# Feeding the mixers un-normed transposed rows, with the bias table's repetition moved from the SyncE queue to a memory-to-memory copy

## The chip, the cores and the metric

The kernel runs on one core of one Trainium2 chip. The metric is the device time of one execution in microseconds; the kernel before has a median of 1729.02 us over 3 runs (1727.54 to 1730.34). The core has TensorE (matmuls and transposes), VectorE, ScalarE and GpSimd for elementwise work, SyncE, which here only issues transfers, and 16 DMA engines that all queues share.

## What is computed

A decoder trunk of two layers on 256 tokens of width 1024, in float32. Each layer: (1) a norm of the residual `h`, one input projection, three token mixers that share it (a diagonal state space scan, latent attention, sparse attention), an output projection; (2) cross-attention into 256 memory tokens `mem`; (3) a SwiGLU channel mixer, dense in layer 0 and with eight experts in layer 1. What the change touches is this:

```python
def rmsnorm(x, g):
    y = xf * lax.rsqrt(jnp.mean(xf * xf, axis=-1, keepdims=True) + EPS)
    return (y * g.astype(jnp.float32)).astype(x.dtype)
...
for l in range(DEPTH):
    proj = rmsnorm(h, mix_norm[l]) @ w_in[l]
    u, cq, ckv, kr, nq, nkv, ngate = jnp.split(proj, offsets, axis=-1)
    y_ssm = ssm_mixer(u, ...)      # complex powers of a, scan over tokens
    y_mla = mla_mixer(cq, ckv, kr, ...)
    y_nsa = nsa_mixer(nq, nkv, ngate, ..., rel_bias)   # scores get head_bias(q_pos - k_pos)
    h = h + concat(norms of y) @ w_out[l]
    h = h + cross_attn(h, mem, ...)
    h = h + (swiglu or moe)(rmsnorm(h, ffn_norm[l]))
```

The scale of the norm is one number per token, so it commutes with the projection: it can be applied to `h` before or to `proj` after.

## The kernel before, in words

**Products and weight chunks.** Every product of the large matrices is made in three matmuls of rounded operands (`split_product`, L456 to L458): each operand is an upper part (rounded) and a lower part (the rest). Weights come in chunks of 1 MB into a ring of six slots, all issued by SyncE, in order, each once the slot's last user is done (semaphore `weights_used`). For each chunk ScalarE writes the upper part (`layer_chunk_upper`, L476) and VectorE the lower part (`layer_chunk_lower`, L480); TensorE waits for the lower one in `split_chunk`. The upper part of chunk c also waits for the user of chunk c-2. Engines run their instructions strictly in the order written; nothing reorders the work.

**Input of a layer.** The squares of `h` (ScalarE L1673 in layer 0, VectorE L1898 in layer 1), a mean, a power on GpSimd (L2350) and a scaling by `rstd` give `row`; TensorE turns it into columns (L1232, 16 transposes `hT0` to `hT3` into banks 0 to 3); ScalarE and VectorE evict the columns times `mix_norm` as upper (`colr`, L1642) and lower (`coll`, L1908) part. Then come the jobs `u`, `zA`, `zB`, `q0`, `q1` (chunks 0 to 4), `ck` and `cv` (chunk 5) and `vs` (chunk 6). Each job is 48 matmuls. Banks go round in fives, each job waiting until the bank's last job is drained.

**After the jobs.** TensorE makes `hid` (L1375, the compression of the sparse group) and `bu0` (L1339, the scan's input). VectorE writes `memr` (L2078), the lower part of the memory columns, in place over `memraw`, then drains `hid`, then does `states(0)` (from 76.5 us in the rows) and so on to the scores.

**GpSimd, layer 0.** Two powers, and a table of complex powers by doubling (`tables`, then `double(1)` to `double(128)`, six operations each over 8m elements, L2350; it needs the sines of L1654). After the last doubling it issues two transfers: `mem_cols` (the memory columns to memory, L2394, `memory_columns` in the profile, 1 MB; semaphore `mem_kept`, for which `memr` waits) and `btab` (L2397), a skewed read of the bias. Both go by GpSimd's own queue.

**The bias.** A small matmul (L1301) makes 6 rows of 384 numbers, VectorE copies them to `biasrow` in SBUF, and SyncE writes each row 128 times to `scratch` in memory (L1195, `skewed_bias`), ahead of chunk 6 in SyncE's queue.

**Between the layers.** The last dense product adds into banks 0 to 3, VectorE adds them to `h` (L943, four times 128x512), and the input of layer 1 begins. ScalarE copies the next layer's powers from `row` and `col` into `big` there (L1681, L1682).

Of the kernel before, what the change touches and what calls it, by code (L numbers as in the profile page):

```python
# [84 lines left out]
JOBS = []  # L85

# [7 lines left out]
for _i, (_n, _e) in enumerate((("u", "act"), ("zA", "act"), ("zB", "act"), ("q0", "dve"), ("q1", "dve"))):  # L94
    _job(_n, _e, _i)
_job("ck", "act")
# [99 lines left out]
def trunk(nc, x, mem, weights, lparams, consts, onehot, relb, fgain, out, scratch, routed, expert_out, mem_cols):  # L196
    with ExitStack() as ctx:
# [50 lines left out]
        eight = sb("eight", [P, 16])  # L248

# [8 lines left out]
        colr = over("colr", [P, KD, T], "col")  # L258
        memr = over("memr", [P, KD, T], "memraw")
# [32 lines left out]
        ftab = big  # L292
# [40 lines left out]
        xsc = small[:, 440:442]  # L333

# [15 lines left out]
        s_out = sem("s_out")  # L350
        bias_back = sem("bias_back")
        mem_kept = sem("mem_kept")
# [21 lines left out]
        row_ready = lsem("row_ready")  # L374
        mem_upper = lsem("mem_upper")
# [45 lines left out]
        def bank(name):  # L421
            return banks[index(name) % ROT]
# [84 lines left out]
        def dense_pe(pe, last_rows, last_columns):  # L507
# [32 lines left out]
            def down(i, n, start=False, last=False):  # L540
                q = f0 + (3 * i + 2 if last else 3 * i + 4)
                pe.wait_ge(split_done, 3 * n + (3 if last else 5))
                pe.wait_ge(hT_done, n + 1)
                up, lo = upper[:, third(q), :], lower[:, q % RING, :]
                for f in range(2):
                    for t in range(TT):
                        x = slice(f * T + t * P, f * T + (t + 1) * P)
                        for nn in range(2):
                            w = slice(f * 1024 + nn * 512, f * 1024 + (nn + 1) * 512)
                            ins = split_product(pe, banks[2 * t + nn][:, :], htu[:, i % 2, x], htl[:, i % 2, x],  # L550
                                                up[:, w], lo[:, w], start and f == 0, last and f == 1)
                ins.then_inc(weights_used, 1)
# [19 lines left out]
            down(n, n, last=True)  # L572
            pe.wait_ge(weights_used, RING + LAYER_CHUNKS)
# [52 lines left out]
        def moe_pe(pe, m, used, first):  # L626
# [34 lines left out]
            def gather_first():  # L661

                pe.wait_ge(row_ready[1], 6)
# [231 lines left out]
        def dense_dve(dve, last_half, next_angles):  # L895
# [37 lines left out]
            step(1, 2 * e + 1, e)  # L933
            step(DENSE_PIECES - 3, DENSE_PIECES - 3)
            step(DENSE_PIECES - 2, DENSE_PIECES - 2, chunks=1)
            units(DENSE_PIECES - 1, DENSE_PIECES - 1)
            for c in range(2):
                layer_chunk_lower(dve, 1, c)
            dve.wait_ge(weights_used, RING + LAYER_CHUNKS)
            for t in range(TT):  # L940
                for n in range(2):
# [160 lines left out]
        def moe_pool(pool, m, tile):  # L1102
# [12 lines left out]
            pool.wait_ge(row_ready[1], 6)  # L1115
# [101 lines left out]
        def _(pe):  # L1217
# [82 lines left out]
            pe.wait_ge(p_dve, 1)  # L1300
            mm(banks[7][0:NH, 0:384], pt[0:33, 1, 0:NH], pt[0:33, 0, 0:384], start=True, stop=True).then_inc(p_pe, 1)  # L1301
            pe.wait_ge(cst_landed, 16)

            def turn_memory(i):

                if i == 0:
                    pe.wait_ge(p_dve, 2)
                    pe.wait_ge(p_act, 3)
                if i == 3:
                    pe.wait_ge(p_act, 4)  # L1310
# [6 lines left out]
            for l in range(L):  # L1317
                pe.wait_ge(row_ready[l], 2)
                transpose_rows("h")
                features_out("u", 0, colr, coll, "h")  # L1320
                narrow_tokens_out("zA", 1, colr, coll)
                narrow_tokens_out("zB", 2, colr, coll)
                features_out("q0", 3, colr, coll)
# [3 lines left out]
                features_out("q1", 4, colr, coll)  # L1327
                if l == 0:
                    turn_memory(3)
                for v, name in enumerate(("ck", "cv")):  # L1330
                    half_features_out(name, 5, v, colr, coll)
                narrow_tokens_out("vs", 6, colr, coll)
# [168 lines left out]
                for i in range(HEADS):  # L1501
                    if scored_at(i):
                        scores(*scored_at(i))
                    if i in MEMK:
                        if MEMK[i] == 0:
                            pe.wait_ge(mem_split[l], KD)
                        features_out(f"mk{MEMK[i]}", MEM_FIRST + MEMK[i], colr, memr)
# [25 lines left out]
                tokens_out("mv0", MEM_VALUES, colr, memr)  # L1533
                tokens_out("mv1", MEM_VALUES + 2, colr, memr, (0,))
                pe.wait_ge(row_ready[l], 4)
                transpose_rows("y", row, (0, 1))
                tokens_out("mv1", MEM_VALUES + 2, colr, memr, (1,))
# [63 lines left out]
                if l == 0:  # L1601
                    wait_drained(pe, l, "fT1")
                    dense_pe(pe, last_rows, last_columns)
# [14 lines left out]
        def _(act):  # L1618
# [11 lines left out]

            def scale_rows(n):

                act.wait_ge(rstd_ready[l], n)
                A(row[:, 0, :], h[:, 0, :], ACT.Copy, scale=rstd[:, 0:1]).then_inc(row_ready[l], 1)
# [36 lines left out]
            act.wait_ge(x_landed, 16)  # L1671
            for t in range(TT):
                ins = A(xkf[:, t * D:(t + 1) * D], h[:, t, :], ACT.Square, accum_out=ss[:, t:t + 1])  # L1673
            ins.then_inc(p_act, 1)
            trigonometry(0)

            for l in range(L):
                if l:
                    act.wait_ge(weights_used, RING + LAYER_CHUNKS)
                    act.wait_ge(ftab_ready[l], 1)  # L1680
                    A(bigf[:, 2048:4096], rowf, ACT.Copy).then_inc(ftab_ready[l], 1)  # L1681
                    A(bigf[:, 0:2048], colf, ACT.Copy).then_inc(ftab_ready[l], 1)  # L1682
                    act.wait_ge(ftab_ready[l], 3)
                    scale_rows(1)
                else:
                    layer_chunk_upper(act, 0, 0)
                transposes_upper(l, "h", C_MIX)
                if l == 0:
                    layer_chunk_upper(act, 0, 1)
                wait_tile(act, l, "u")  # L1690
                layer_chunk_upper(act, l, 2)
                drained(A(uT[:, :, :], bank("u")[:, :], ACT.Copy))
                wait_tile(act, l, "zA")
                layer_chunk_upper(act, l, 3)
                drained(A(z[:, :, 0:256], bank("zA")[:, :].rearrange("p (t n) -> p t n", t=2), ACT.Copy))
# [3 lines left out]
                A(z[:, :, 256:352], b[:, :, 0:96], ACT.Copy)  # L1699
                A(gates, b[:, :, 96:114], ACT.Tanh, scale=0.5)  # L1700
                drained(A(kwr[:, :, :], b[:, :, 114:242], ACT.Copy))
# [10 lines left out]
                wait_tile(act, l, "ck")  # L1712
                for gi in range(2):
                    b = bank("ck")[gi * 64:(gi + 1) * 64, 0:T]
                    A(kc[0:64, 0, gi, :], b, ACT.Copy)
                    ins = A(kc[64:128, 0, gi, 0:255], b[:, 1:256], ACT.Copy)
                drained(ins)
# [8 lines left out]
                else:  # L1726
                    act.wait_ge(p_act, 7)
                for k in range(KD):
                    A(colr[:, k, :], memraw[:, k, :], ACT.Copy, scale=cols[:, C_MEM + k:C_MEM + k + 1]).then_inc(mem_upper[l], 1)
# [5 lines left out]
                act.wait_ge(ftab_ready[l], 2 * l + 1)  # L1735
# [142 lines left out]
        def _(dve):  # L1878
# [34 lines left out]
            def norm_h(junk, l):  # L1913
                for t in range(TT):
                    if l:
                        dve.wait_ge(ffn_added, 2 * t + 2)
                    ins = squares(h[:, t, :], junk[:, t * D:(t + 1) * D], ss[:, t:t + 1])
                link(ins)
                mean_eps(0, 2, D).then_inc(ss_ready[l], 1)

            def scale_rows(n):

                dve.wait_ge(rstd_ready[l], n)
                if l:
                    dve.wait_ge(ftab_ready[l], 3)
                dve.tensor_scalar(row[:, 1, :], h[:, 1, :], rstd[:, 1:2], None, ALU.mult).then_inc(row_ready[l], 1)

# [27 lines left out]
            angles(0)  # L1955
            dve.wait_ge(bias_landed, 32)
            dve.tensor_scalar(pt[0:33, 1, 0:NH], pt[0:33, 1, 0:NH], 8.0, None, ALU.mult).then_inc(p_dve, 1)

            for l in range(L):
                if l:  # L1960
                    norm_h(xkf, l)
                    scale_rows(1)
                else:
                    dve.wait_ge(p_act, 1)
                    mean_eps(0, 2, D).then_inc(ss_ready[l], 1)
                    dve.wait_ge(rstd_ready[l], 1)
                    for t in range(TT):
                        dve.tensor_scalar(row[:, t, :], h[:, t, :], rstd[:, t:t + 1], None, ALU.mult).then_inc(row_ready[l], 1)
                    dve.wait_ge(p_pe, 1)
                    dve.tensor_copy(biasrow, banks[7][0:NH, 0:384]).then_inc(p_dve, 1)  # L1970
                    layer_chunk_lower(dve, l, 0)
                transposes_lower("h", coll, C_MIX, 0)
                if l == 0:
                    layer_chunk_lower(dve, l, 1)
# [663 lines left out]
```

## Time and profile before

| | |
|---|---|
| median of 3 runs | 1729.02 us |
| the profiled execution's own time | 1730.89 us |
| its span, first to last instruction | 1729.1 us |
| mean granted TensorE clock | 0.982 of full speed |
| TensorE matmul busy | 1660.1 us, 96% |
| VectorE / ScalarE / GpSimd busy | 1347.5 / 1087.3 / 225.2 us |

All times below are microseconds from the span's start in that one execution. A matmul's ends are modelled, so that TensorE's waits are read from the engine that released it and from the chain of work, not from its busy share.

### The profile page before, as it was taken

The numbers are of one execution on the slowest core, as the hardware profiler recorded it, in microseconds if no ns is written. First come the engines' busy times: TensorE is split into PE (matmuls) and PEld (weight loads), VectorE is DVE, ScalarE is ACT, GpSimd is POOL, SyncE is SP. The second block draws the span as 40 slices with busy tenths as digits, with TensorE's granted clock in tenths as the row PEclk, the third lists the DMA queues.
The fourth block names the chain that finished last, engine by engine and source line by source line (L and its number), as shares of the span: only waits on it lengthen the run. The fifth ranks groups of instructions, "written<-read, shape, count | busy, mean of one in ns | idle before, by whom it ended". The sixth has DMA issues, their size and how long they took to land.

```text
span 1729.1 us, 24273 instructions
## 1 busy us (share of the span) xinstructions
PE 1660.1 (96%) x8480; PEld 1386.1 (80%) x8480; DVE 1347.5 (78%) x1501; ACT 1087.3 (63%) x1195; POOL 225.2 (13%) x235
## 2 busy tenths in 40 slices
PE   7899999999799999999999999999999999999995
PEld 6788888888697888878888888888888888888783
DVE  7676656445667756678988988988989889889895
ACT  5455544445445554367777777777777777777773
POOL 7443001003603500040000000000000000000200
PEclk9889999999998999989999999999999999999998
DMA  8602526855440234379999999999999999999992
GB/s 297 239 25 74 181 111 232 337 179 189 170 147 25 74 128 165 122 281 399 377 373 378 379 381 374 370 391 372 385 375 376 384 371 362 388 373 360 418 372 75
DMA packets 68111, 475.94 MB, mean 275 GB/s; under 512 B 7533, under 2 KB 8301, under 8 KB 13390
## 3 DMA queue, kind: packets, MB, share of 16 engines
q1 hardware_dynamic: 62790, 452.11, 68.7%
q0 software_dynamic: 5024, 22.86, 3.4%
q8 instruction: 39, 0.64, 0.1%
q10 hardware_dynamic: 232, 0.12, 0.0%
q14 instruction: 26, 0.21, 0.0%
HBM read 461.82 MB, written 13.24 MB: 275 GB/s over the span
## 4 chain that ended last, share of the span: by engine, by line
PE 83%; DVE 6%; ACT 4%; DMA 4%; issue 2%; POOL 0%; DVEq 0%; POOLq 0%; ACTq 0%; SPq 0%
PE bank L456 24%; PE bank L458 24%; PE bank L457 24%; DMA ring<-in_weights 3%; ACT upper L499 1%; PE bank L647 1%; DVE lower L480 1%; ACT upper L476 1%; PE bank L1339 1%; PE bank L1554 1%; DVE xel L1014 1%; PE bank L1455 1%; DVE lower L505 1%; PE bank L1513 1%; PE bank L1232 1%
## 5 line engine op out<-in xcount | busy, mean ns | idle before, releaser
L505 DVE TENSOR_TENSOR lower<-ring,upper 128x2048 fp32r<-128x2048 f32 x369 | 849.3, 2302 | 145.0 <-ACT upper L499 132.2
L499 ACT ACTIVATE upper<-ring 128x2048 fp32r<-128x2048 f32 x369 | 706.2, 1914 | 113.5 <-PE bank L458 100.9
L456 PE MATMUL bank<-upper,xeu 128*128 128x512 f32 x896 | 360.0, 402 | 3.5 <-DVE lower L505 3.5
L458 PE MATMUL bank<-upper,xel 128*128 128x512 f32 x896 | 350.5, 391 | 0.0
L457 PE MATMUL bank<-lower,xeu 128*128 128x512 f32 x896 | 349.5, 390 | 0.0
L456 PE MATMUL bank<-upper,htu 128*128 128x512 f32 x536 | 209.9, 392 | 4.9 <-DVE htl L1030 3.4
L458 PE MATMUL bank<-upper,htl 128*128 128x512 f32 x536 | 208.7, 389 | 0.0
L457 PE MATMUL bank<-lower,htu 128*128 128x512 f32 x536 | 208.6, 389 | 0.0
L456 PEld LDWEIGHTS bank<-upper,xeu 128*128 128x128 f32 x896 | 168.3, 188 | 36.3 <-DVE lower L505 5.1
L458 PEld LDWEIGHTS bank<-upper,xel 128*128 128x128 f32 x896 | 168.2, 188 | 36.0
L457 PEld LDWEIGHTS bank<-lower,xeu 128*128 128x128 f32 x896 | 168.7, 188 | 31.7
L480 DVE TENSOR_TENSOR lower<-ring,upper 128x2048 fp32r<-128x2048 f32 x42 | 96.7, 2303 | 64.7 <-ACT upper L476 64.3
L456 PEld LDWEIGHTS bank<-upper,htu 128*128 128x128 f32 x536 | 100.6, 188 | 30.9 <-issue 10.5
L476 ACT ACTIVATE upper<-ring 128x2048 fp32r<-128x2048 f32 x42 | 80.3, 1911 | 62.8 <-PE bank L458 62.8
L458 PEld LDWEIGHTS bank<-upper,htl 128*128 128x128 f32 x536 | 100.6, 188 | 21.1
L457 PEld LDWEIGHTS bank<-lower,htu 128*128 128x128 f32 x536 | 100.6, 188 | 20.5
L458 PE MATMUL bank<-colr,lower 128*128 128x256 f32 x384 | 108.7, 283 | 0.0
L824 ACT ACTIVATE htu<-bank 128x256 fp32r<-128x256 f32 x112 | 43.5, 388 | 97.1 <-PE bank L647 96.6
L820 ACT ACTIVATE big<-bank 128x256 f32<-128x256 f32 x112 | 43.0, 384 | 63.8 <-PE bank L458 63.8
L457 PE MATMUL bank<-lower,colr 128*128 128x512 f32 (+1 forms) x224 | 77.9, 348 | 0.0
L458 PE MATMUL bank<-upper,coll 128*128 128x512 f32 (+1 forms) x208 | 77.7, 374 | 0.0
L456 PE MATMUL bank<-colr,upper 128*128 128x256 f32 x256 | 74.4, 291 | 2.7 <-DVE xor L1908 1.8
(387 smaller groups left out, 2474.5 us busy)
## 6 DMA issues: line engine op xcount, KB each, us to landing
ring<-in_weights SPq DMA_DIRECT2D x423, 1024.0 KB, 5.6
routed_rows<-g POOLq DMA_DIRECT2D x1, 4096.0 KB, 36.6
lp<-in_lparams POOLq DMA_DIRECT2D x1, 3634.5 KB, 14.4
lp<-in_lparams SPq DMA_DIRECT2D x1, 3584.0 KB, 35.6
memraw<-routed_rows POOLq DMA_DIRECT2D x7, 512.0 KB, 8.0
expert_rows<-xk POOLq DMA_DIRECT2D x7, 512.0 KB, 9.0
skewed_bias<-vm SPq DMA_DIRECT2D x1, 1152.0 KB
h<-in_x SPq DMA_DIRECT2D x1, 1024.0 KB, 5.7
```

Of the source, the lines that this page charges most:

```text
L456: pe.matmul(to, x_up, w_up, start=start, stop=False, skip_group_check=True)
L457: pe.matmul(to, x_up, w_lo, start=False, stop=False, skip_group_check=True)
L458: return pe.matmul(to, x_lo, w_up, start=False, stop=stop, skip_group_check=True)
L476: act.activation(upper_slot(c), ring[:, c % RING, :], ACT.Copy).then_inc(wt_upper[l], 1)
L480: dve.tensor_tensor(lower[:, c % RING, :], ring[:, c % RING, :], f32(upper_slot(c)), ALU.subtract).then_inc(wt_split[l], 1)
L499: act.activation(upper[:, third(q), :], ring[:, q % RING, :], ACT.Copy).then_inc(done, 1)
L505: dve.tensor_tensor(lower[:, q % RING, :], ring[:, q % RING, :], f32(upper[:, third(q), :]), ALU.subtract).then_inc(done, 1)
L647: ins = pe.transpose(banks[2][:, f * P:(f + 1) * P], hr[:, i % 2, 0, f * P:(f + 1) * P], ident)
L820: act.activation(gs[:, i % 2, 0, :], banks[i % 2][:, 0:256], ACT.Silu).then_inc(m["silu"], 1)
L824: act.activation(htu[:, i % 2, 0:256], banks[2][:, 0:256], ACT.Copy).then_inc(m["ht_up"], 1)
L1014: ins = dve.scalar_tensor_tensor(xel[buf][:, k, :], banks[5 + k // 4][:, (k % 4) * P:(k % 4 + 1) * P], cols[:, C_FFN + k:C_FFN + k + 1], f ...
L1232: ins = pe.transpose(b[:, (k * TT + t) * P:(k * TT + t + 1) * P], src[:, t, f:f + P], ident)
```

## The change

- `h` is turned as it is; `rstd` goes to the drains. A diagonal of `rstd` times a matrix of ones gives a row of it in every partition (`rows_bc`): two matmuls put between `zA` and `zB`, after which VectorE copies the row, drains `u`, and only then makes chunk 2's lower part.
- The turned columns get banks 5, 6, 7, 4, and in layer 1 another place (`bigr` in `big`), so that one of ScalarE's table copies goes. `ck` and `u` are drained by VectorE instead of ScalarE.
- The last dense product goes bank by bank, with the adds and the transposes behind each.
- The bias rows go to memory once (`biasline`); GpSimd repeats them from memory to memory, ahead of `double(64)`.
- In layer 0 the squares, the sines, the factors (L1984 and the lines around it) and the powers on GpSimd come in another order; in layer 1 the factors are made within the dense stage. SyncE loads the identity, then `x`, chunk 0, the other constants.

```diff
 # SyncE
+            sp.dma_start(ident, consts[:, 0:P]).then_inc(cst_landed, 16)
             sp.dma_start(h[:, :, :], x...).then_inc(x_landed, 16)
-            sp.dma_start(cst[:, :], consts).then_inc(cst_landed, 16)
...
                 load(s, s)
+                if s == 0:
+                    sp.wait_ge(cst_landed, 16)
+                    sp.dma_start(cst[:, P:], consts[:, P:]).then_inc(cst_landed, 16)
...
             sp.wait_ge(p_dve, 2)
-            sp.dma_start(scratch[:, :, :], biasrow.unsqueeze(1).broadcast_to([NH, P, 384])).then_inc(s_scr, 16)
+            sp.dma_start(biasline[:, :], biasrow).then_inc(s_scr, 16)
             load(RING, RING)
 # TensorE, per layer
-                pe.wait_ge(row_ready[l], 2)
-                transpose_rows("h")
+                if l == 0:
+                    pe.wait_ge(x_landed, 16)
+                    transpose_rows("h", h)
+                    ... the bias matmul, into bank 3
+                else:
+                    last_down()
+                    for n in range(2):
+                        for t in range(TT):
+                            pe.wait_ge(ffn_added, 2 * n + t + 1)
+                            turn_blocks("h", h, (2 * n, 2 * n + 1), t)
+                features_out("u", 0, xh, coll, "h")
+                narrow_tokens_out("zA", 1, xh, coll)
+                pe.wait_ge(diagonal_ready[l], 1)
+                for t in range(TT):
+                    ins = mm(banks[5][:, t * P:(t + 1) * P], ones, pt[:, 0, t * P:(t + 1) * P], start=True, stop=True)
+                ins.then_inc(rows_spread[l], 1)
+                narrow_tokens_out("zB", 2, xh, coll)
 # ScalarE, layer 0
+                    transposes_upper(l, "h", C_MIX, (0, 1))
                     layer_chunk_upper(act, 0, 0)
+                    transposes_upper(l, "h", C_MIX, (2, 3))
+                    trigonometry(0)
+                    layer_chunk_upper(act, 0, 1)
+                    row_squares()
 # VectorE, per layer
+                layer_chunk_lower(dve, l, 1)
+                dve.wait_ge(squared[l], 1)
+                mean_eps(0, 2, D).then_inc(ss_ready[l], 1)
+                if l == 0:
+                    input_factors(0)
+                dve.wait_ge(rstd_ready[l], 1)
+                dve.tensor_scalar(rstd_half, rstd[:, 0:2], 0.5, None, ALU.mult)
+                for t in range(TT):
+                    ins = dve.tensor_scalar(pt[:, 0, t * P:(t + 1) * P], ident, rstd[:, t:t + 1], None, ALU.mult)
+                ins.then_inc(diagonal_ready[l], 1)
+                dve.wait_ge(rows_spread[l], 1)
+                spread = dve.tensor_copy(rows_bc[:, :], banks[5][:, 0:T])
...
+                wait_tile(dve, l, "u")
+                drained(tt(uT[:, :, :], bank("u")[:, :]..., rows_bc[:, :]..., ALU.mult))
+                layer_chunk_lower(dve, l, 2)
+                if l == 0:
+                    ... the squares of the memory rows
+                layer_chunk_lower(dve, l, 3)
 # GpSimd, layer 0
+                    tables(0, *ftab[0], kTf[:, 512:])
+                    for m in (1, 2, 4):
+                        link(double(m))
                 pool.wait_ge(ss_ready[l], 1)
                 power(0, 2, rstd_ready[l])
-                    tables(0, ftab[:, 0], ftab[:, 1], kTf[:, 512:])
-                    for m in (1, 2, 4, 8, 16, 32):
+                    for m in (8, 16, 32):
                         link(double(m))
                     pool.wait_ge(p_dve, 3)
                     power(6, 2, p_pool)
+                    pool.wait_ge(s_scr, 16)
+                    pool.dma_start(scratch[:, :, :], biasline.unsqueeze(1).broadcast_to([NH, P, 384])).then_inc(bias_spread, 16)
                     link(double(64))
                 ...
                     double(128).then_inc(ftab_ready[l], 1)
                     pool.dma_start(mem_cols, memrawf).then_inc(mem_kept, 16)
-                    pool.wait_ge(s_scr, 16)
+                    pool.wait_ge(bias_spread, 16)
                     pool.dma_start(btab[:, :, :], skew).then_inc(bias_back, 16)
```

## Rows read from the trace of the kernel before

**Rows 1.** The page: shares of the chain that ended last.
```profile
PE 83%; DVE 6%; ACT 4%; DMA 4%; issue 2%; POOL 0%; DVEq 0%; POOLq 0%; ACTq 0%; SPq 0%
```

**Rows 2.** The chain in order of time, its longest pieces: start, length, what.
```profile
21.69 35.06 DMA ring<-in_weights
...
58.71 2.30 DVE lower L480
```

**Rows 3.** Stretches: length, busy PE, PEld, DVE, ACT, POOL, clock, DMA share, GB/s.
```profile
25.00:32.00 7.00, 7.00 (x61) 7.00 (x60) 6.62 (x17) 2.40 (x2) 6.68 (x10) 1.00 0.39 61
53.40:61.00 7.60, 0.00 (x0) 0.00 (x0) 2.29 (x2) 4.21 (x7) 5.55 (x4) 0.65 0.82 326
```

**Rows 4.** Timeline of SyncE's queue; then DMA packets by size, 26:31, 52:54, 54:56.
```profile
11.65 0.95 SPq L1195 DMA_DIRECT2D skewed_bias<-vm  x1
21.69 9.50 SPq L1182 DMA_DIRECT2D ring<-in_weights  x1
...
DMA packets 172, 0.26 MB, mean 53 GB/s; under 512 B 0, under 2 KB 172, under 8 KB 172
q1 hardware_dynamic: 172, 0.26, 34.5%
...
DMA packets 100, 0.50 MB, mean 248 GB/s; under 512 B 16, under 2 KB 45, under 8 KB 45
...
DMA packets 101, 0.79 MB, mean 395 GB/s; under 512 B 7, under 2 KB 7, under 8 KB 7
```

**Rows 5.** Timeline of VectorE: start, length, instructions, idle before and its releaser.
```profile
69.20 0.69 DVE L2054 COPY vs<-bank 128x512 f32<-128x512 f32 x1
71.11 3.26 DVE L2078 SCALAR_TENSOR_TENSOR memr<-memraw,lp,colr 128x256 fp32r<-128x256 f32 x8 [1.22 <-DMA memory_columns<-memraw]
75.49 0.22 DVE L2083 COPY rt<-bank 64x1 f32<-64x1 f32 x2 [1.12 <-PE bank L1375]
76.55 1.29 DVE L1895 TENSOR_TENSOR lp<-bank,big 128x512 f32<-128x512 f32 x2 [0.41 <-PE bank L1339]
```

**Rows 6.** Timelines of ScalarE and GpSimd, layer 0's opening.
```profile
8.76 1.28 ACT L1653 ACT_TABLE_LOAD   x1
...
10.43 0.19 POOL L2363 COPY big<-small 128x8 f32<-128x8 f32 x1 [0.73 <-ACT small L1654]
12.53 2.13 POOL L2350 TENSOR_TENSOR big<-big 128x16 f32<-128x16 f32 x1
14.62 0.21 POOL L2350 TENSOR_TENSOR g<-big 128x16 f32<-128x16 f32 x1
56.13 2.35 POOL L2350 TENSOR_TENSOR big<-big,attn 128x1024 f32<-128x1024 f32 x1
60.45 0.78 POOL L2394 DMA_DIRECT2D memory_columns<-memraw  x1 [1.98 <-ACT memraw L1664]
```

**Rows 7.** DMA issues: KB each, median us to landing.
```profile
h<-in_x SPq DMA_DIRECT2D x1, 1024.0 KB, 5.7
memory_columns<-memraw POOLq DMA_DIRECT2D x1, 1024.0 KB, 10.6
out<-row SPq DMA_DIRECT2D x1, 1024.0 KB, 4.0
```

**Rows 8.** Timelines of TensorE, VectorE, ScalarE where layer 1 begins.
```profile
448.08 0.60 PE L537 MATMUL bank<-cst,big 128*128 128x128 f32 x4
...
467.30 2.48 DVE L943 TENSOR_TENSOR h<-h,bank 128x512 f32<-128x512 f32 x4 [0.30 <-PE bank L458]
474.46 3.65 PE L1232 MATMUL bank<-cst,row 128*128 128x128 f32 x16 [7.20 <-ACT row L1634]
475.58 3.40 ACT L1642 ACTIVATE colr<-bank,lp 128x256 fp32r<-128x256 f32 x8 [1.27 <-PE bank L1232]
484.36 1.92 ACT L476 ACTIVATE colu<-ring 128x2048 fp32r<-128x2048 f32 x1 [5.38 <-PE bank L458]
490.12 1.92 ACT L476 ACTIVATE upper<-ring 128x2048 fp32r<-128x2048 f32 x1 [3.36 <-PE bank L458]
```

More of the change, by code:

```diff
@@ L571, in dense_pe, with last_down @@
             turn(n, n)
-            down(n, n, last=True)
-            pe.wait_ge(weights_used, RING + LAYER_CHUNKS)
+            def last_down():
+                q = f0 + 3 * n + 2
+                pe.wait_ge(split_done, 3 * n + 3)
+                pe.wait_ge(hT_done, n + 1)
+                up, lo = upper[:, third(q), :], lower[:, q % RING, :]
+                for nn in range(2):
+                    for t in range(TT):
+                        for f in range(2):
+                            x = slice(f * T + t * P, f * T + (t + 1) * P)
+                            w = slice(f * 1024 + nn * 512, f * 1024 + (nn + 1) * 512)
+                            ins = split_product(pe, banks[2 * t + nn][:, :], htu[:, n % 2, x], htl[:, n % 2, x],
+                                                up[:, w], lo[:, w], False, f == 1)
+                        ins.then_inc(weights_used if (nn, t) == (1, TT - 1) else dense_done, 1)
+            return last_down
         lg = bigf[:, 3072:3088].rearrange("p (t e) -> p t e", t=TT)
@@ L1953, in angles, with input_factors @@
                 dve.tensor_scalar(ab, ab, 1.0, math.pi / 2, ALU.mult, ALU.add).then_inc(par_ready[l], 1)
[L1955 to L1974, printed above, removed]
-                    dve.wait_ge(mem_landed, 16)
-                    for t in range(TT):
-                        link(squares(memrows[:, t, :], btabf[:, 0:D], ss[:, 6 + t:7 + t]))
-                    mean_eps(6, 2, D).then_inc(p_dve, 1)
-                layer_chunk_lower(dve, l, 2)
+            def input_factors(l):
                 tt(den, lr, lr, ALU.mult)
@@ L1996, in _ @@
                 link(tt(fi, fi, den, ALU.mult))
+            angles(0)
+            dve.wait_ge(bias_landed, 32)
+            dve.tensor_scalar(pt[0:33, 1, 0:NH], pt[0:33, 1, 0:NH], 8.0, None, ALU.mult).then_inc(p_dve, 1)
+            for l in range(L):
+                xh = columns[l]
+                if l:
+                    transposes_lower("h", coll, C_MIX, 0, up=xh)
+                else:
+                    transposes_lower("h", coll, C_MIX, 0, (0, 1))
+                    layer_chunk_lower(dve, l, 0)
+                    transposes_lower("h", coll, C_MIX, 0, (2, 3))
+                    dve.wait_ge(p_pe, 1)
+                    dve.tensor_copy(biasrow, banks[3][0:NH, 0:384]).then_inc(p_dve, 1)
+                layer_chunk_lower(dve, l, 1)
[5 more added lines that the diff above has]
+                dve.tensor_scalar(rstd_half, rstd[:, 0:2], 0.5, None, ALU.mult)
+                for t in range(TT):
+                    ins = dve.tensor_scalar(pt[:, 0, t * P:(t + 1) * P], ident, rstd[:, t:t + 1], None, ALU.mult)
+                ins.then_inc(diagonal_ready[l], 1)
+                dve.wait_ge(rows_spread[l], 1)
+                spread = dve.tensor_copy(rows_bc[:, :], banks[5][:, 0:T])
+                if l == 0:
+                    spread.then_inc(rows_read, 1)
+                    dve.wait_ge(rows_read, 1)
+                else:
+                    link(spread)
+                wait_tile(dve, l, "u")
+                drained(tt(uT[:, :, :], bank("u")[:, :].rearrange("p (c n) -> p c n", c=2),
+                           rows_bc[:, :].unsqueeze(1).broadcast_to([P, 2, T]), ALU.mult))
+                layer_chunk_lower(dve, l, 2)
+                if l == 0:
+                    dve.wait_ge(mem_landed, 16)
+                    for t in range(TT):
+                        link(squares(memrows[:, t, :], btabf[:, 0:D], ss[:, 6 + t:7 + t]))
+                    mean_eps(6, 2, D).then_inc(p_dve, 1)
                 layer_chunk_lower(dve, l, 3)
@@ L2053, in _ @@
                 wait_tile(dve, l, "vs")
-                drained(dve.tensor_copy(vs[:, :, :], bank("vs")[:, :].rearrange("p (t n) -> p t n", t=2)))
+                for t in range(TT):
+                    ins = dve.tensor_scalar(vs[:, t, :], bank("vs")[:, t * 256:(t + 1) * 256], rstd[:, t:t + 1], None, ALU.mult)
+                drained(ins)
                 def states(j):
```

191 lines of the change are left out of this document (97 added, 94 removed).

## The prediction, as it was made before the run

> **What bounds the kernel now.** I read the page's chain of work first: TensorE is 83% of it [rows 1]. So only places where that chain leaves TensorE can give or cost time, and the edits lie at two of them: the opening of layer 0 and the change of layers. I then asked for the chain in order of time, for stretches, and for each engine's timeline around both places.
>
> *Opening.* The longest single piece of the chain is the load of weight chunk 6: issued at 21.69, landed 35.06 us later [rows 2]. `vs` needs it, and TensorE does nothing in 53.4 to 61.0 [rows 3]. The reader should see why it was late. In 25 to 32 the DMA engines move 61 GB/s at a share of 0.39 [rows 3]. In 26 to 31 all 172 packets are under 2 KB (0.26 MB, 1.5 KB each: the bias rows), and they occupy 34.5% of 16 engines, 5.5 engines' worth [rows 4]. The destination is [6, 128, 384]: six engines carry it, 6 x 128 = 768 packets. Chunk 6 stands behind it in the same queue; SyncE even needs 9.50 us to issue it. Such packets are gone between 54 and 56 (45 - 16 = 29 in 52:54, 7 - 7 = 0 after) [rows 4], and then chunk 6 lands.
>
> But VectorE, not TensorE, leads what follows. It has drained `vs` at 69.9 and waits for `memory_columns` until 71.11, writes `memr` for 3.26, waits 1.12 for L1375, and begins `states(0)` at 76.55 [rows 5]. The transfer it waited for comes last in GpSimd's chain: doublings until 58.48, a wait of 1.98 for the memory columns, issue at 60.45 [rows 6], 10.6 to landing [rows 7]. So there are two limits 1 to 2 us apart, and the change removes the first.
>
> *Change of layers.* The last dense matmul ends at 467.3. Four adds, the squares, the power and the scaling follow one another until the transposes at 474.46 [rows 8]: 7.2 us without TensorE.
>
> **The change of layers, step by step.**
> Removed: squares, power and scaling ahead of the transposes. The last dense product is bank by bank, so three of the four adds (2.48 / 4 = 0.62 each [rows 8]) go beside it and the fourth ends at about 468.0. Twelve transposes need not wait for it. After a busy TensorE one takes 0.60 / 4 = 0.15 at most, and 3.65 / 16 = 0.23 now [rows 8]; all are done by about 469.2. ScalarE evicts from 468.0 at 3.40 / 8 = 0.43 per column block, VectorE 0.9 behind it, so the last lower block is there at 472.3, and `u` ends 24 matmuls after the first half, at about 475.9. Before, it ended just ahead of ScalarE's chunk 2 at 484.36, say 484.0 [rows 8]. Gain 8.1. ScalarE's table copy that remains fits ahead of 468, as the one that goes did not have to; the factors put into the dense stage hide beside its matmuls, since there VectorE waits for ScalarE before most chunks (at nothing; uncovered they would be 2.5 us).
>
> Added: a wait that takes part of it back. `zB` needs chunk 2's lower part, and VectorE is written to make that only after the spread row, which TensorE makes only after `zA`. From the end of `zA` (475.9 + 490.12 - 484.36 = 481.7): two matmuls 0.3, a copy of 256 elements 0.45, `u` drained 0.7 (512 elements, as `vs` 0.69 [rows 5]), some 0.1 of links, the lower part 2.3 [rows 2]. TensorE idles about 3.9 us. All behind `zB` on TensorE waits with it; none did before. Net +8.1 - 3.9 = +4.2 for layer 1 (bounds +1.8, if the pause brings the lower clock and its 2.4, and +5). `ck`, and products in place of copies, add about 3 us of work to VectorE, which has as much room before `vs`, as the factors are gone from there.
>
> **The opening, step by step.**
> Same stall of 3.9 between `zA` and `zB`, against 2 us gained by turning `x` before its squares. Chunk 6 now meets a queue with only 9 KB of bias ahead; it should land at about 26 to 30, and `vs` ends at about 61.3 instead of 69.2. Were TensorE the limit, that would be 7.9.
>
> GpSimd's chain is what counts. It starts after the sines. These now follow the transposes of `x`, all eight evictions and chunk 0 on ScalarE. `x` is there at about 6.9 (5.7 to landing [rows 7], issued behind the identity), its first columns at 7.9 (four transposes at 0.23); 8 x 0.43 for the evictions, 1.9 for chunk 0, 1.8 for the sines with their table load of 1.28 [rows 6] make 15.0, against 10.43: 4.6 later. From there to 58.48: a power in the middle +0.7, the issue of the repetition +0.9 (as 0.78 [rows 6]). Beside a lower part on VectorE a GpSimd operation of 0.21 took 2.13 [rows 6]: chunk 0's no longer meets the doublings (-1.9), chunk 6's now does (+2.1). The doublings end at 58.48 + 6.4 = 64.9, and `memory_columns` goes out at about 65. Landing takes 4.0 (1 MB, quiet queues) to 10.6 [rows 7]: 69 to 76.
>
> Now the repetition itself: still 768 packets, issued by GpSimd at about 41, ahead of `memory_columns` in the same queue. Nothing in the trace shows a memory-to-memory copy; the nearest rows are the old transfer's, from about 24.5 to 54, 29.5 us [rows 3, 4]. From below, at 172 packets in 5 us, 22.3 us. From above, 29.5 plus four 1 MB weight chunks sharing the engines at some 2.6 us each: 40. It ends at 41 + 22 to 41 + 40 = 63 to 81, and where it ends last the columns behind it land some 3.5 later. I take the old transfer's 29.5 and half of the sharing, as the shape is the same: end 73, landing T = 76.5.
>
> In the Trainium skill, page "DMA: Bandwidth & Descriptors", section "Why a DMA increments its semaphore by 16 and not by 1", a transfer is split over the largest count up to 16 that divides its outermost dimension, from either kind of queue; by that rule the copy again has six engines. The trace agrees for the old transfer (5.5 engines' worth); no row shows it for GpSimd's queue.
>
> Then `states(0)` begins at T + 3.26 + 0.9 = 80.7, against 76.55: a loss of 4.1. Besides, TensorE has little to do between 68 and 80, and may return at its lower clock. After the pause of 53.4 to 61.0 (mean 0.65 [rows 3]: the lower level, 1.2 GHz, in part of it) `vs` took from 61.0 to 69.2, 8.2, where a job takes 490.12 - 484.36 = 5.76 [rows 2, 5, 8]: 2.4 dearer. So 0 to 2.4; I take 2.
>
> **Sum.** +4.2 - 4.1 - 2.0 = -1.9, a loss. Against the profiled execution's own 1730.89 (span 1729.1) that is 1732.8; that execution lies 1.87 above the median, so on the median 1729.02 + 1.9 = 1730.9.
>
> **Rivals.**
> *Fast: the repetition is out of the way.* It has 16 engines or is quick from memory, and T is 70 to 72. Then layer 0 gives 76.55 - T - 4.2 = +2.3 to +0.3, layer 1 +4.2: 1722.5 to 1725. For it: 16 engines would need 48 packets each. Against it: the unchanged shape. Could the full 7.9 + 4.2 = 12 come (1717)? Only if `memory_columns` landed by 65, when it is about to be issued.
> *Slow: the repetition holds the columns.* From memory to memory each packet reads and writes memory, and shares six engines with weight chunks: end 81 or later, T = 84 to 87, so layer 0 loses 12 to 15, with the clock's 2 and layer 1's 4.2: 1739 to 1742. It decides from T = 78.0 (4.2 = T - 72.35 + 2 - 3.46 turned slower by over 0.2%). For it: 81 is my upper bound. Against: chunks come in bursts with pauses.
> *No change:* the wait for `zB` absent or doubled by a fall of the clock, the rest at zero: within 2 us of 1729.
>
> **How the numbers follow.** A measurement of this kernel tells 0.2% (3.46 us) from no change. Likeliest, T 73 to 78: chance 0.38, 1727.4 to 1732.4, all within 0.2%. No change: 0.03, within it too. Fast: 0.26, faster. Slow, from T = 78 on: 0.33, slower. So faster 0.26, same 0.41, slower 0.33. The range leaves 2 in 10 outside, the far ends of fast and slow: 1723 to 1739.
>
> **What would show it right or wrong.** Chunk 6 landed by 30 and no idle TensorE before `vs`; TensorE idle 3 to 5 us ahead of `zB` in both layers, with VectorE at L480's chunk 2 as releaser; `u` of layer 1 ending 8 us after the last dense matmul's end; GpSimd's last doubling ending at 63 to 67; packets of 1.5 KB in GpSimd's queue until past 65 on about six engines; VectorE's `memr` waiting for `memory_columns`, the longest wait of the opening. Wrong if those packets are over by 55, if GpSimd ends before 60, or if VectorE's own load sets `states(0)`.

## The result, and the profile after

The changed kernel takes 1737.13 us (median of 16 runs, 1730.88 to 1740.39) and the kernel before, beside it, 1729.83 (16 runs, 1727.54 to 1731.9): ratio 1.004, 95% interval 1.0034 to 1.0047. It is 7.3 us slower. The prediction said 1730.9 with a range of 1723 to 1739: the range holds the time, the single figure is 6.2 too low, and "within 0.2%" was the wrong one of the three outcomes. The profiled execution of after took 1736.06 (span 1734.2) against 1730.89 (span 1729.1), so the profile has 5.2 of the 7.3 to explain.

The method below is to look for one event in both traces and to see how the distance between them changes along the span. Four events do: the start of `states(0)`, the last dense matmul, ScalarE's chunk 2 of layer 1 (the end of `u`), and its chunk 4 of layer 1 (the end of `zB`).

**Layer 0's opening: 3.0 later.** The timeline of VectorE in after, where [rows 5] answer to it (start, length, instructions, idle before and its releaser):

```profile
58.53 2.00 DVE L1940 TENSOR_TENSOR rt<-row,cst 128x32 f32<-128x32 f32 x2
60.57 2.34 DVE L1940 TENSOR_TENSOR row<-rt 128x32 f32<-128x32 f32 x1
62.95 2.41 DVE L1940 TENSOR_TENSOR rt<-row,cst 128x32 f32<-128x32 f32 x2
65.39 0.19 DVE L1940 TENSOR_TENSOR row<-rt 128x32 f32<-128x32 f32 x1
...
66.83 3.47 DVE L1940 TENSOR_TENSOR attn<-bank,rows_bc 64x256 f32<-64x256 f32 x8
...
73.68 3.26 DVE L2130 SCALAR_TENSOR_TENSOR memr<-memraw,lp,colr 128x256 fp32r<-128x256 f32 x8 [0.21 <-DMA memory_columns<-memraw]
...
79.52 1.29 DVE L1940 TENSOR_TENSOR lp<-bank,big 128x512 f32<-128x512 f32 x2 [1.36 <-PE bank L1386]
```

`states(0)` starts at 79.52 against 76.55. The wait for `memory_columns` before `memr` is only 0.21, where it was 1.22; the columns are not what is late. The reader should look at the rotation of the shared key's rows (four groups of 128x32): it takes 7.05, from 58.53 to 65.58. In the kernel before it ran after the last doubling (58.48), in 1.07, from 60.92 to 61.99:

```profile
60.92 0.29 DVE L1895 TENSOR_TENSOR rt<-row,cst 128x32 f32<-128x32 f32 x2
...
61.80 0.19 DVE L1895 TENSOR_TENSOR row<-rt 128x32 f32<-128x32 f32 x1
```

Behind it the drains of the banks end at 70.3. The chain of after in order of time (start, length, what) shows that these drains now hold the end:

```profile
40.23 3.27 DVE lower L493
...
69.87 0.44 DVE attn L1940
70.45 7.03 PE bank L1422 x64
77.47 2.01 PE bank L1386 x4
```

From 40.2 to 70.3 the chain is VectorE's, but for 0.2. Then come TensorE's 64 matmuls of `hid`, which wait for the last drain, and the four of `bu0`. The same pieces of the chain before, then the stretch 70 to 75, before and after (length, busy PE, PEld, DVE, ACT, POOL, clock, DMA share, GB/s):

```profile
70.25 5.20 PE bank L1375 x64
75.45 1.07 PE bank L1339 x4
```

```profile
70.00:75.00 5.00, 5.00 (x64) 4.83 (x63) 3.26 (x8) 4.96 (x11) 0.00 (x0) 1.00 0.75 261
```

```profile
70.00:75.00 5.00, 4.55 (x43) 4.58 (x44) 4.69 (x13) 2.22 (x3) 0.00 (x0) 0.50 0.92 374
```

So `hid` begins only 0.2 later than before. The other 2.8 of the 3.0 are the clock: TensorE has worked for only 1.41 of 65 to 70, the granted clock is 0.50 in the next stretch, and the two products take 7.03 and 2.01 where they took 5.20 and 1.07. GpSimd's timeline and the issues of DMA (KB, us to landing) answer to [rows 6, 7]:

```profile
62.83 2.38 POOL L2402 TENSOR_TENSOR big<-big,attn 128x1024 f32<-128x1024 f32 x1
65.15 0.67 POOL L2451 DMA_DIRECT2D memory_columns<-memraw  x1
```

```profile
skewed_bias<-bias_rows POOLq DMA_DIRECT2D x1, 1152.0 KB, 16.7
memory_columns<-memraw POOLq DMA_DIRECT2D x1, 1024.0 KB, 8.5
```

The doublings end at 65.2 (predicted 64.9). The repetition lands 16.7 after its issue at 36.9, long before the columns go out, not after 29.5 or more. Chunk 6 is issued at 21.08 and lands 7.6 later.

**Dense stage: 5 later still.** The last dense matmul ended at 467.3 before; in after TensorE's transposes follow it at 475.17, 8 later. 2.6 of that come from layer 0 (the lower part behind its attention stands at 158.45 against 155.90). The rest has one place, which the timeline of VectorE shows:

```profile
433.24 0.67 DVE L1940 TENSOR_TENSOR small<-lp 128x8 f32<-128x8 f32 x2
...
437.13 1.99 DVE L1940 TENSOR_TENSOR small<-small 128x8 f32<-128x8 f32 x2
...
440.25 2.46 DVE L1940 TENSOR_TENSOR small<-small 128x8 f32<-128x8 f32 x2
442.74 0.69 DVE L937 TENSOR_TENSOR htl<-bank,htu 128x512 fp32r<-128x512 f32 x1
```

These are the 15 small operations of `input_factors(1)`: 9.5 us from 433.24 to 442.74. TensorE's next matmul starts at 443.58 after 3.65 of waiting for `htl`. In the stretch 440 to 445 TensorE is busy for 1.42 of 5, at a granted clock of 0.86, and the clock is 0.80 in the next one, where both are 1.00 in the kernel before (length, busy PE, PEld, DVE, ACT, POOL, clock, DMA share, GB/s):

```profile
440.00:445.00 5.00, 1.42 (x4) 1.17 (x5) 4.90 (x6) 2.24 (x2) 4.84 (x5) 0.86 0.62 210
445.00:450.00 5.00, 5.00 (x19) 4.08 (x18) 5.00 (x4) 0.00 (x0) 5.00 (x2) 0.80 0.00 0
```

**Change of layers: 8.3 gained, 5.6 given back.** Timelines of TensorE, VectorE and ScalarE, in answer to [rows 8], then the stretch 495 to 500:

```profile
475.17 1.91 PE L1265 MATMUL bank<-cst,h 128*128 128x128 f32 x16
...
493.68 0.39 PE L469 MATMUL bank<-colu,bigr 128*128 128x256 f32 x1 [3.44 <-DVE lower L493]
```

```profile
475.36 0.69 DVE L973 TENSOR_TENSOR h<-h,bank 128x512 f32<-128x512 f32 x1 [0.67 <-PE bank L471]
...
490.28 0.42 DVE L2028 COPY rows_bc<-bank 128x256 f32<-128x256 f32 x1 [6.50 <-PE bank L1367]
490.74 0.69 DVE L1940 TENSOR_TENSOR uT<-bank,rows_bc 128x512 f32<-128x512 f32 x1
491.34 2.28 DVE L493 TENSOR_TENSOR lower<-ring,colu 128x2048 fp32r<-128x2048 f32 x1
```

```profile
484.15 1.92 ACT L489 ACTIVATE colu<-ring 128x2048 fp32r<-128x2048 f32 x1 [3.03 <-PE bank L471]
489.91 1.91 ACT L489 ACTIVATE upper<-ring 128x2048 fp32r<-128x2048 f32 x1 [3.85 <-PE bank L471]
501.30 1.92 ACT L489 ACTIVATE colu<-ring 128x2048 fp32r<-128x2048 f32 x1 [8.75 <-PE bank L471]
```

```profile
495.00:500.00 5.00, 5.00 (x32) 5.00 (x31) 0.83 (x1) 0.00 (x0) 0.00 (x0) 0.68 0.00 0
```

After a dense stage that ends 8 later, `u` ends at 484.15, 0.2 earlier than before: 8.3 gained. Then `zB` ends at 501.30 against 495.88: 17.15 after `u` instead of 11.52, so 5.6 lost. From the end of `zA` (489.91) to the first matmul of `zB` (493.68) pass 3.8: the two matmuls of the spread row and the pause of 3.44. `zB` itself then takes 7.6 instead of 5.76, at a clock of 0.68 in the stretch 495 to 500: 1.9 more. From there the two traces stay 5.1 to 5.4 apart to the last write.

### The profile page after: what moved, and what is told of

Read it like the earlier page. It is cut to its first block, busy times and chain, and to the rows that moved or that the text cites. A ratio compares the mean times of both kernels' runs of the same rounds, so it can differ in the third digit from the quotient of the medians.

```text
span 1734.2 us, 24306 instructions
## 1 busy us (share of the span) xinstructions
PE 1665.6 (96%) x8488; PEld 1391.5 (80%) x8488; DVE 1361.9 (79%) x1514; ACT 1082.4 (62%) x1195; POOL 219.2 (13%) x236
## 4 chain that ended last, share of the span: by engine, by line
PE 83%; DVE 8%; ACT 4%; issue 2%; DMA 2%; POOL 0%; DVEq 0%; POOLq 0%; SPq 0%; ACTq 0%
PE bank L469 24%; PE bank L471 24%; PE bank L470 24%; DVE lower L493 2%; ACT upper L512 2%; PE bank L674 1%; DMA ring<-in_weights 1%; ACT upper L489 1%; PE bank L1386 1%; PE bank L1601 1%; DVE xel L1044 1%; DVE lower L518 1%; PE bank L1502 1%; PE bank L1422 1%; PE bank L1560 1%
## 5 line engine op out<-in xcount | busy, mean ns | idle before, releaser
L2402 POOL TENSOR_TENSOR small<-small,cst 128x2 f32<-128x2 f32 (+2 forms) x12 | 24.1, 2006 | 417.3 <-DVE small L1946 417.2
L471 PE MATMUL bank<-colr,lower 128*128 128x256 f32 x256 | 73.0, 285 | 0.0
L469 PE MATMUL bank<-upper,colu 128*128 128x512 f32 x176 | 69.6, 395 | 0.0
## 6 DMA issues: line engine op xcount, KB each, us to landing
skewed_bias<-bias_rows POOLq DMA_DIRECT2D x1, 1152.0 KB, 16.7
```

Source lines behind the costliest of these rows:

```text
L469: pe.matmul(to, x_up, w_up, start=start, stop=False, skip_group_check=True)
L471: return pe.matmul(to, x_lo, w_up, start=False, stop=stop, skip_group_check=True)
L2402: return pool.tensor_tensor(out, a, b, op)
```

## The experiments

Each is a small edit of one of the two kernels. Ratios are against the kernel before, run beside it in three sets (its medians 1730.16 for the first four, 1730.37 for old_write to sync_repeat, 1729.52 for the last two).

**factors_idle**: after, with layer 1's factors made outside the dense stage, where VectorE waits for the spread row.

```diff
-dense_dve(dve, last_half, lambda: angles(1), lambda: input_factors(1))
+dense_dve(dve, last_half, lambda: angles(1), lambda: None)
...
 ins.then_inc(diagonal_ready[l], 1)
+if l == 1:
+    input_factors(1)
 dve.wait_ge(rows_spread[l], 1)
```

> The changed kernel, but layer 1's factors are made while VectorE waits for the spread row between zA and zB, instead of in the dense stage. Theory 1 (the factors' small operations each wait for a GpSimd doubling, 9.5 us in all at 433.2 to 442.7, and TensorE waits for L937 behind them, with a fall of its clock): the dense stage gets back 5.5 us, the chain of small operations takes about 2.5, and the time is the changed kernel's less 5.5, about 1731.5. Rival (the factors were covered and the dense stage lost its time elsewhere, to the new order of the last product): 0 to 1 us, about 1736.5.

Measured: 1731.95 (11 runs), ratio 1.0011, 1.0002 to 1.0021: 5.2 below after. The same operations, last of them on VectorE's timeline:

```profile
478.56 0.24 DVE L1940 TENSOR_TENSOR small<-lp 128x8 f32<-128x8 f32 x2
...
480.72 0.37 DVE L1940 TENSOR_TENSOR small<-small 128x8 f32<-128x8 f32 x2
```

They take 2.5 here, with GpSimd idle, against 9.5 beside its doublings. The last add starts at 470.23 instead of 475.36. So 5.1 of the 5.5 us of the dense stage are the place of the factors.

**zb_first**: after, with chunk 2's lower part made ahead of VectorE's wait for the spread row, in both layers.

```diff
+layer_chunk_lower(dve, l, 2)
 dve.wait_ge(rows_spread[l], 1)
...
-layer_chunk_lower(dve, l, 2)
```

> The changed kernel, but VectorE makes chunk 2's lower part before it waits for the spread row. Theory 1 (this wait costs 3.5 us in each layer and the clock's fall behind it some 2 more): zB follows zA with no pause, layer 1 gains 5.6, and layer 0 gains 5.6 before vs, of which VectorE and memory_columns let through 0 to 2: about 1730.5. Rival (the pause only moves to a later wait, as VectorE is full between zB and memr): layer 1 gains under 2 and the time is above 1735.

Measured: 1728.52 (11 runs), ratio 0.9986, 0.9977 to 0.9995: 8.6 below after. ScalarE's timeline around `zA` and `zB`:

```profile
482.48 1.92 ACT L489 ACTIVATE colu<-ring 128x2048 fp32r<-128x2048 f32 x1 [3.02 <-PE bank L471]
...
494.44 1.92 ACT L489 ACTIVATE colu<-ring 128x2048 fp32r<-128x2048 f32 x1 [3.56 <-PE bank L471]
```

`zB` ends 11.96 after `u`, not 17.15, and the stretch 484 to 495 has a clock of 1.00. In layer 1 the pause and its clock cost 5.2; the other 0.4 of the 5.6 stays, as the two matmuls of the spread row do. In layer 0 `zB` comes 11.95 after `u` instead of 17.10, the same 5. But there `u` itself ended 1.6 later in this execution (22.73 against 21.18), from code that is the same in both, so `zB` is 3.6 earlier and `states(0)` 2.0 (77.48): VectorE works there from 39.35 to the end of its drains at 68.3 without an idle gap over 0.2, and is a second limit. The two spans are 6.9 apart, the medians 8.6.

**both**: the two edits together.

> Both edits together. Theory 1: they lie in different stages and add: 1737.1 - 5.5 - 5.6 - (0 to 2) = 1724 to 1726, which is 4 to 6 under the kernel before; TensorE's jobs before zB start where the prediction had them. Rival (they share VectorE's idle stretch in layer 1, so that one takes the other's place): 1729 or more.

Measured: 1722.32 (5 runs), ratio 0.9955, 0.9941 to 0.9969. That is 14.8 below after, where the two single gains make 5.2 + 8.6 = 13.8. They add up. VectorE still rotates rows for 8 (53.97 to 62.1), and the 64 matmuls behind its drains run in 7.03.

**repeat_alone**: the kernel before, with only the new way of repeating the bias: the rows once to memory, then GpSimd's memory-to-memory copy ahead of the doubling from 64.

```diff
-sp.dma_start(scratch[:, :, :], biasrow...broadcast_to([NH, P, 384])).then_inc(s_scr, 16)
+sp.dma_start(biasline[:, :], biasrow).then_inc(s_scr, 16)
...
+pool.wait_ge(s_scr, 16)
+pool.dma_start(scratch[:, :, :], biasline...broadcast_to([NH, P, 384])).then_inc(bias_spread, 16)
 link(double(64))
```

> The kernel before with one part of the change: the bias rows go to memory once and GpSimd repeats them from memory to memory ahead of double(64). Theory of two limits: chunk 6 lands by about 30 and TensorE's pause of 53.4 to 61.0 goes, but states(0) stays with VectorE, the doublings (about 59.5) and memory_columns (landing about 68 to 70), so the gain is 1 to 4 us, 1726 to 1729. Rival (chunk 6 was the limit): 7.5 us or more, under 1722.5. Rival (the repetition holds the columns' transfer): no gain or a loss.

Measured: 1726.95 (12 runs), ratio 0.9979, 0.9969 to 0.9989. This part alone is a gain of 0.2%. VectorE's timeline:

```profile
71.18 3.25 DVE L2079 SCALAR_TENSOR_TENSOR memr<-memraw,lp,colr 128x256 fp32r<-128x256 f32 x8 [2.38 <-DMA memory_columns<-memraw]
```

The 7.6 us without TensorE [rows 3] are gone, and `states(0)` starts at 74.99, only 1.6 earlier. The second limit, GpSimd's doublings and then `memory_columns`, is where the prediction put it: `memr` waits 2.38 for it. But `bu0`, at a clock of 0.50 in 65 to 70, ends at 74.95 too, so a third limit lies beside it.

**old_write**: both, with the repetition undone, SyncE's old write from the rows in the chip's memory.

> The kernel with both edits, with the bias table written as before: SyncE writes each row 128 times from SBUF ahead of chunk 6. Theory of two limits: chunk 6 lands at about 57 again and TensorE waits for vs, but states(0) moves by only 0 to 2 us, as VectorE and the doublings set it near 76; so 1722.3 to 1724.5. Rival (the repetition is what pays): 1727 or more.

Measured: 1722.74 (5 runs), ratio 0.9957, 0.9943 to 0.9971: not told apart from both. Chunk 6 is late again (ScalarE waits 13.33 for the ring), the drains end at 69.0, and `states(0)` starts at 77.03 against 76.03. But `u` of layer 0 ended 0.9 later in this execution (22.16 against 21.22), from the same code, so no gain of the new repetition in the changed kernel is established. What it frees on TensorE is taken elsewhere: with the old write the rotation takes 3.2, not 8, and the 64 matmuls run in 5.28, at a clock of 1.00 in 70 to 75, not in 7.03.

**rotate_late**: both, with the rotation moved behind the drains of the banks.

```diff
-rotate((krp[:, :, 64:80], krp[:, :, 80:96]), ...).then_inc(rope_ready[l], 1)
...
+rotate((krp[:, :, 64:80], krp[:, :, 80:96]), ...).then_inc(rope_ready[l], 1)
 dve.wait_ge(lp_landed, 16)
```

> The kernel with both edits (1722.3), and VectorE's rotation of the key columns (six small operations with two operands in SBUF) moved behind the drains of q1, ck and cv. Theory (such an operation waits for the GpSimd operation it meets, up to 2.4 us each beside the 1024-element doublings, while drains from a bank do not; so the rotation costs 8.1 us in 54.0 to 62.1 instead of 1.1, and VectorE is then the limit of layer 0's opening): the drains run at once, most of the rotation falls behind the last doubling (64.3), states(0) comes 1 to 3 us earlier: about 1720.5. Rival (the limit is memory_columns or TensorE's hid): within 0.5 us of 1722.3.

Measured: 1719.75 (5 runs), ratio 0.9942, 0.9928 to 0.9955. VectorE's and GpSimd's timelines side by side:

```profile
56.30 3.47 DVE L1940 TENSOR_TENSOR attn<-bank,rows_bc 64x256 f32<-64x256 f32 x8
59.81 0.90 DVE L1940 TENSOR_TENSOR rt<-row,cst 128x32 f32<-128x32 f32 x2
60.75 2.31 DVE L1940 TENSOR_TENSOR row<-rt 128x32 f32<-128x32 f32 x1
63.09 2.38 DVE L1940 TENSOR_TENSOR rt<-row,cst 128x32 f32<-128x32 f32 x2
```

```profile
58.65 1.91 POOL L2404 TENSOR_TENSOR attn<-big 128x1024 f32<-128x1024 f32 x1
60.64 2.36 POOL L2404 TENSOR_TENSOR big<-big,g 128x1024 f32<-128x1024 f32 x1
62.96 2.35 POOL L2404 TENSOR_TENSOR big<-big,attn 128x1024 f32<-128x1024 f32 x1
```

The drains, which read a bank, keep their 0.43 each beside GpSimd. The rotation, whose operands both lie outside the banks, waits for GpSimd's operations wherever it stands: each of these three groups ends within 0.2 of the end of one of GpSimd's operations. And TensorE needs its result:

```profile
65.75 0.47 PE L1406 MATMUL bank<-cst,row 128*128 128x128 f32 x1 [3.88 <-DVE row L1940]
67.22 7.06 PE L1422 MATMUL bank<-attn,lp 128*64 128x45 f32 x64
```

So `hid` begins no earlier than in both (66.96), and at the lower clock again. `states(0)` doesn't move (76.12; `u` of layer 0 ended 0.8 later than in both), `u` of layer 1 ends 1.9 earlier (475.65 against 477.55), and the two intervals overlap.

**rotate_columns**: rotate_late, with ScalarE issuing `memory_columns`.

> As rotate_late, and ScalarE issues memory_columns itself, right after it has drained the memory columns, instead of GpSimd after the last doubling. Theory (with the rotation late the transfer that lands near 69 to 70 is the next limit): it lands near 60, memr does not wait, another 0 to 1.5 us below rotate_late. Rival (VectorE's own work up to vs is the limit): the same as rotate_late within 0.5 us.

Measured: 1721.82 (5 runs), ratio 0.9955, 0.9941 to 0.9969. `memr` no longer waits (67.89), `states(0)` starts at 74.90, 1.2 earlier (0.8 of it from the start: `u` of layer 0 ends at 21.25 against 22.01), and the time is no better: no gain established.

**sync_repeat**: the kernel before, with the rows once to memory and the repetition issued by SyncE from there, ahead of chunk 6.

```diff
+sp.dma_start(biasline[:, :], biasrow).then_inc(s_scr, 16)
+sp.wait_ge(s_scr, 16)
+sp.dma_start(scratch[:, :, :], biasline...broadcast_to([NH, P, 384])).then_inc(bias_spread, 16)
 load(RING, RING)
```

> The kernel before, with the rows written once and repeated from memory to memory, but by SyncE, ahead of chunk 6, where repeat_alone has GpSimd do it. Theory A (the queue of issue decides: SyncE's keeps the six engines and packets of 1.5 KB, GpSimd's regrouped them into 252 packets of 4.5 KB): the repetition takes 25 us or more again, chunk 6 lands after 50, and the time is that of the kernel before within 2 us, 1728 to 1731. Theory B (the source decides: memory rather than 6 partitions of SBUF): it takes under 18 us and chunk 6 lands by 45, the time as repeat_alone, about 1727.

Measured: 1727.45 (11 runs), ratio 0.9981, 0.9972 to 0.999. SyncE's queue, and the DMA packets of 26 to 31, the stretch of [rows 4]:

```profile
25.37 0.86 SPq L1198 DMA_DIRECT2D skewed_bias<-bias_rows  x1
```

```profile
DMA packets 379, 0.65 MB, mean 130 GB/s; under 512 B 0, under 2 KB 369, under 8 KB 369
```

The same destination and the same queue as before, but 379 packets in 5 us where 172 went. Small packets are over soon after 36 (16 in 36 to 41), some 10 after the issue, where the old transfer took 29.5. `states(0)` starts at 71.27, 5.3 earlier, and the span is 1723.8, 5.3 shorter; the median is 2.9 below the 1730.37 of the kernel before beside it, and the ratio is not told apart from repeat_alone's. Against repeat_alone `memory_columns` lands earlier (`memr` does not wait, 67.54) and the 64 matmuls take 5.24, at a clock of 1.00. Not the queue but the source made the old transfer slow.

**sync_rotate** and **sync_columns**: rotate_late with that repetition by SyncE, and in the second ScalarE issuing `memory_columns`.

> The kernel of rotate_late, with its memory-to-memory repetition of the bias rows issued by SyncE ahead of chunk 6, as in sync_repeat, instead of by GpSimd ahead of the doubling from 64. Theory (the source of the copy decides, and GpSimd's own issue of it, 1.35 us, and the small packets it makes stand in the way): chunk 6 still lands before its use at about 42 us, the doublings end some 1.3 us earlier, memory_columns lands before VectorE asks for it, and the first states of the memory start at 73 to 75 us instead of 76.12. Time 1 to 3 us below rotate_late, which is about 1717 to 1719. Rival (the span is set by the clock and the later stages, so an earlier opening no longer shows): within 1 us of rotate_late. Rival on the other side: SyncE waits for the rows to come back from memory and for the repetition, so that chunk 6 and the rest of the ring are late and TensorE stands still near 42 us: 3 us or more above rotate_late.

> As sync_rotate, and ScalarE issues memory_columns after its last part of the memory's norm instead of GpSimd after its last doubling, as in rotate_columns. If memory_columns has landed in time in sync_rotate already, this is within 0.1 per cent of it; if VectorE still waits there for the columns, it is 1 us below. Rival from rotate_columns (the transfer of the columns then shares the DMA engines with the ring's chunks and btab): about 2 us above sync_rotate.

Measured: 1720.34 (5 runs), ratio 0.9945, 0.9931 to 0.9958, and 1719.79 (5 runs), 0.9938, 0.9924 to 0.9952. In sync_rotate `states(0)` starts at 72.34, 3.8 before rotate_late (1.0 of it from the start of the layer), its 64 matmuls take 5.91 instead of 7.06, and `u` of layer 1 ends at 471.40, 4.3 before. Its span is 1716.7. The median doesn't show it: by time the two, and rotate_late, are not told apart. All three are about 0.6% faster than the kernel before and 1% faster than after.

## Why the prediction came out as it did

The terms, in the order of the sum (positive is gained):

| Step | predicted | profiled |
|---|---|---|
| layer 1: turned input, `u` after the last dense matmul | +8.1 | +8.3 |
| layer 1: two matmuls and the pause before `zB` | -3.9 | -3.8 |
| layer 1: lower clock behind it | 0, bound -2.4 | -1.9 |
| factors in the dense stage | 0 ("uncovered 2.5") | -5.5 |
| layer 0: the wait ahead of `states(0)` | -4.1 | -0.2 |
| layer 0: lower clock | -2.0 | -2.8 |

The terms that were profiled make -5.9. Layer 0's loss is 2.6 by its attention, which makes -5.5, and the spans are 5.1 apart. Two errors stand against each other: the factors and layer 1's clock cost 7.4 more than the sum had, the opening about 3 less. The range held the time by luck: it reached up to 1739 for the slow rival, whose mechanism did not come.

**The step that failed: the factors priced at nothing.** I wrote that "the factors put into the dense stage hide beside its matmuls, since there VectorE waits for ScalarE before most chunks (at nothing; uncovered they would be 2.5 us)". Those waits exist, 1.11 to 2.7 each, but beside GpSimd's doublings the 15 operations take 9.5, and no wait covers that. Both bounds were wrong, since 2.5 was the duration on a quiet machine. factors_idle gives 5.2 back by time. I had the evidence: [rows 6] show a GpSimd operation of 0.21 that took 2.13 beside a lower part, and I used it only for GpSimd, not for VectorE's small operations in the other direction.

**The change of layers was right.** The gain is within 0.2. The pause stood where it was put, and with its two matmuls it is within 0.1. The clock's share was named as a bound and left out of the sum; it came, in this layer as in the other. zb_first shows pause and clock together as 5.2.

**The opening was wrong in its first term.** The doublings ended at 65.2 (64.9), though their parts differ: the issue of the repetition took 1.35, not 0.9, and GpSimd waited 1.44 for VectorE ahead of it. Turning `x` early gained 0.6, not 2 (`u` ends at 21.18 against 21.78). The repetition was mis-sized: 16.7 to landing instead of 29.5 to 40, so it never held the columns, which landed by 73.7 (76.5 predicted). That is the likeliest band of the prediction, near the fast rival's 72. The recorded sum has a slip there as well: 41, the old 29.5 and half of the sharing (5.2) make 75.7, not 73, and with 3.5 more T is 79.2 and the time 1733.6, past its own bound for "slower".

The columns were then not what `states(0)` waited for, so the loss of 4.1 by them did not come. VectorE's own load, 7.05 of rotation instead of 1.1, kept the start of `hid` at 70.45 (70.25 before), and the lower clock, priced at 2.0, cost 2.8. Two of the things that I had named as proving the step wrong are there: the repetition over by 55 (at 53.6), and VectorE's own load. The outcome of the slow rival, slower, came without its mechanism.

Left open: 2.1 of the 7.3 between the medians are not in the two profiled executions (5.2 apart). After's runs spread over 9.5, before's over 4.4. sync_rotate shows the same from the other side, a shorter profiled span without a shorter median. Part of it may lie at the very start, where `u` of layer 0 ended at 21.18 in after and at 22.73 in zb_first with the same code before it; no run here shows how much.

## What to carry to other kernels

Before small operations are moved into the "free" time of an engine, look at what the engine next to it does in that stretch: a duration measured beside an idle neighbour is no upper bound. A product whose statistics are applied later buys its time only if nothing behind it needs the late factor in queue order; here one lower part written behind that wait took back 5 of 8. Where two limits lie 1 to 2 us apart, removing the first moves the stage behind them by about their distance (1.6 in repeat_alone), and a version that removes both is needed to see the rest. And a gain of some us in one profiled execution is not yet a gain: sync_repeat's and sync_rotate's medians don't show theirs in full.

## What the runs showed of the hardware

**Small operations of VectorE beside GpSimd.** Operations of 128x8 that take 0.17 to 0.20 alone took up to 1.25 beside GpSimd's of 128x512 (1.05 to 1.27 each), and groups of 128x32 took 2.0 to 2.4 beside its of 128x1024 (1.9 to 2.4, one of 3.96): the ends of the long ones lie within 0.2 of the end of one of the neighbour's. Drains from a bank kept 0.43. The Trainium skill, page "SBUF — State Buffer", section "SBUF: two separate sides", has the two engines share one pair of ports as an exclusive lock for a whole instruction, which VectorE needs where both inputs lie in SBUF; the traces agree, with these durations.

**The source of a broadcast copy.** 768 rows of 1.5 KB to [6, 128, 384] took 29.5 read from SBUF and some 10 read from memory, from the same queue. From GpSimd's queue the copy came in other packets, and in 15.5 to 17.8. Packets and bytes of that queue in after, in 39 to 44 and in 49 to 54:

```profile
q0 software_dynamic: 464, 0.36, 24.6%
...
q0 software_dynamic: 79, 0.33, 16.2%
```

First 0.8 KB each on average, most under 512 B, then 4.2 KB each, and at 24.6% of 16 engines, 3.9 engines' worth (32.0%, 5.1 engines' worth, in repeat_alone in 39 to 44).

**Short pauses and the clock.** After TensorE stood for 3.44 before `zB`, the granted clock of 495 to 500 was 0.68 of full speed, a mean between its two levels, 2.4 and 1.2 GHz, and `zB` took 1.9 longer. With the pause gone it stayed at 1.00. In the opening of after TensorE was busy for 1.41 of 65 to 70 (clock 0.81); the clock of the next two stretches of 5 was 0.50, the lower level, and 64 matmuls with 45 columns took 7.03 instead of 5.20, 1.35 times as long, while the four of `bu0` (256 columns) took 2.01 instead of 1.07.
